# Attention weights summed over key tiles on GpSimd ahead of two matmuls with ones, in a one-core hybrid decoder layer

## What is computed

```
s = einsum('bhtd,bhsd->bhts', q, k) * w_ts
num = decay * einsum('bhtd,bhdv->bhtv', q, c_prev) + einsum('bhts,bhsv->bhtv', s, v)
den = decay * einsum('bhtd,bhd->bht', q, n_prev) + sum(s, axis=-1)
h = num / maximum(abs(den), exp(-m_t))
c_new = carry * c_prev + einsum('bhs,bhsd,bhsv->bhdv', g, k, v)
n_new = carry * n_prev + einsum('bhs,bhsd->bhd', g, k)
```

## Time and profile before

| | us |
|---|---|
| median of three runs | 1762.06 (1760.64 to 1764.90) |
| the profiled execution, its own time | 1765.68 |
| its span, first to last instruction | 1763.9 |
| TensorE busy | 1732.0 (98%) |
| VectorE busy | 1174.0 (67%) |
| ScalarE busy | 743.5 (42%) |
| GpSimd busy | 435.0 (25%) |
| mean granted clock of TensorE | 0.992 of full |

### The profile page before, as it was taken

How to read it: one execution, slowest core, us unless ns; L and a number is a source line. 1 busy time by engine, 2 the same in 40 slices (tenths; PEclk the granted TensorE clock), 3 DMA queues, 4 the chain that set the end, 5 groups by cost and what they waited for, 6 DMA issues and landing times.

```text
span 1763.9 us, 37199 instructions
## 1 busy us (share of the span) xinstructions
PE 1732.0 (98%) x13831; PEld 1717.0 (97%) x13831; DVE 1174.0 (67%) x1832; ACT 743.5 (42%) x867; POOL 435.0 (25%) x382
## 2 busy tenths in 40 slices
PE   8989999999999999999999999999999999999997
PEld 6889999999999999999999999999999999999997
DVE  3575765748576574857677887777545777777553
ACT  5533433443343344334344555544434333334443
POOL 3341421415142141514211222222000222222000
PEclk8999999999999999999999999999999999999998
DMA  7668678776857777686766566565666666666663
GB/s 185 161 158 205 161 210 195 192 199 177 208 153 212 188 201 193 184 202 161 201 176 180 161 188 179 173 181 170 181 185 182 179 178 178 179 176 178 178 173 107
DMA packets 591091, 318.79 MB, mean 181 GB/s; under 512 B 16771, under 2 KB 585603, under 8 KB 588907
## 3 DMA queue, kind: packets, MB, share of 16 engines
q1 hardware_dynamic: 576016, 292.66, 60.8%
q10 hardware_dynamic: 14555, 23.50, 5.2%
q0 software_dynamic: 432, 1.31, 0.3%
HBM read 305.07 MB, written 12.78 MB: 180 GB/s over the span
## 4 chain that ended last, share of the span: by engine, by line
PE 94%; DMA 2%; DVE 1%; ACT 1%; POOL 1%; issue 1%; SPq 0%; ACTq 0%; DVEq 0%; POOLq 0%
PE strip L1302 60%; PE strip L1307 30%; PE aux L1210 1%; PE aux L1395 1%; PE strip L1239 1%; PE aux L1399 1%; DMA x_tok<-in_x_prompt 1%; DMA scratch_q<-qkd 0%; PE aux L1256 0%; DVE w_lo L841 0%; PE aux L1371 0%; DMA rb<-scratch_rows 0%; PE strip L1249 0%; ACT w_hi L582 0%; PE aux L1408 0%
## 5 line engine op out<-in xcount | busy, mean ns | idle before, releaser
L841 DVE TENSOR_TENSOR w_lo<-w_raw,w_hi 128x1024 fp32r<-128x1024 f32 x556 | 715.4, 1289 | 382.5 <-ACT w_hi L582 379.9
L582 ACT ACTIVATE w_hi<-w_raw 128x1024 fp32r<-128x1024 f32 x560 | 592.7, 1060 | 883.6 <-PE strip L1307 846.6
L1302 PE MATMUL strip<-xh,w_hi 128*128 128x266 f32 (+2 forms) x3424 | 870.6, 288 | 1.5 <-ACT w_hi L582 1.5
L1302 PE MATMUL strip<-xl,w_hi 128*128 128x266 f32 (+2 forms) x3424 | 866.6, 287 | 0.0
L1302 PEld LDWEIGHTS strip<-xh,w_hi 128*128 128x128 f32 x3424 | 646.5, 189 | 2.3 <-ACT w_hi L582 1.6
L1302 PEld LDWEIGHTS strip<-xl,w_hi 128*128 128x128 f32 x3424 | 645.9, 189 | 0.3
L1307 PE MATMUL strip<-xh,w_lo 128*128 128x266 f32 (+2 forms) x3424 | 494.7, 287 | 3.5 <-DVE w_lo L841 3.5
L1307 PEld LDWEIGHTS strip<-xh,w_lo 128*128 128x128 f32 x3424 | 451.8, 189 | 3.9 <-DVE w_lo L841 3.9
L1302 PE MATMUL strip<-hh,w_hi 128*128 128x264 f32 x704 | 176.2, 286 | 0.0
L1302 PE MATMUL strip<-hl,w_hi 128*128 128x264 f32 x704 | 174.7, 283 | 0.0
L566 POOL TENSOR_TENSOR gg<-sg,cz 128x264 f32<-128x264 f32 x44 | 58.3, 1326 | 411.8 <-ACT sg L786 411.8
(11 more groups left out here) (284 smaller groups left out, 1247.3 us busy)
## 6 DMA issues: line engine op xcount, KB each, us to landing
w_raw<-in_w_in SPq DMA_DIRECT2D x256, 512.0 KB, 4.3
w_raw<-in_w_up SPq DMA_DIRECT2D x176, 512.0 KB, 4.0
w_raw<-in_w_down SPq DMA_DIRECT2D x64, 512.0 KB, 4.1
w_raw<-in_w_out SPq DMA_DIRECT2D x32, 512.0 KB, 4.1
w_raw<-in_w_down SPq DMA_DIRECT2D x32, 384.0 KB, 3.4
c_st<-in_state_mlstm_C ACTq DMA_DIRECT2D x8, 1024.0 KB, 11.1
out<-c_st ACTq DMA_DIRECT2D x8, 1024.0 KB, 6.9
rb<-scratch_rows ACTq DMA_DIRECT2D x8, 270.0 KB, 4.7
```

The source lines that it names most:

```text
L582: act.activation(w_hi[:, slot, :], w_raw[:, slot, :], ACT.Copy).then_inc(hi_done, 1)
L841: v.tensor_tensor(w_lo[:, slot, :], w_raw[:, slot, :], w_hi[:, slot, :].bitcast(f32), ALU.subtract).then_inc(lo_done, 1)
L1302: pe.matmul(bank[b][:, 0:c1 - c0], w_hi[:, slot, w], xt[:, k0 + k, c0:c1], start=(first and k == 0 and t == 0), stop=False)
```

## The change

On TensorE the three accumulating matmuls with ones over `pt`, and the one over `qp`, go. In their place GpSimd adds the key tiles of `pt` by query into `wx`, appends the product of sample queries and new `n` as 8 more columns, and splits the 266 columns into `p_hi` and `p_lo`, both fp32r. TensorE multiplies each with ones, after the matmuls for the new state, and waits for GpSimd before that. `p_hi` lies in the space of `arg`, `p_lo` in that of `wx`. The four small operations for the samples' `n` move from VectorE to GpSimd, three of them ahead of the wait for exp. The denominators of prompt and samples are taken in one pass of 266 columns, for which the rows in `rb` change order, and the three small operations at `i` = 22 go. `conv_state()` moves from behind the mask to the start of head 0's `back`, ahead of the wait for `rb`.

```diff
@@ gpsimd, back(n, first) @@
+                if first:
+                    conv_state()
                 g.wait_ge(rb_in, n * 16 + 16)
 ...
+                g.tensor_tensor(sn[:, :], scn[...], dec, ALU.mult).then_inc(sn_done, 1)
+                g.wait_ge(qkd_done, n * 3 + 3)
+                g.wait_ge(sn_done, n * 2 + 1)
+                g.tensor_tensor(sn[:, :], sn[:, :], qkd[:, :, 1], ALU.add).then_inc(sn_done, 1)
+                g.wait_ge(sn_done, n * 2 + 2)
+                g.tensor_tensor(n_new[...], sn[:, :], ones[:, 0:NS], ALU.mult).then_inc(n_kept, 1)
                 g.wait_ge(exp_done, n + 1)
                 g.tensor_tensor(g3[:, :], wx[:, WG:WN], scale_t[:, 0:3], ALU.mult).then_inc(g3_done, 1)
                 g.tensor_tensor(wx[:, 0:WG], wx[:, 0:WG], mask[:, 0:WG], ALU.mult).then_inc(masked, 1)
-                if first:
-                    conv_state()
 ...
                     g.tensor_tensor(cu[:, :], us[:, :], cgs[:, :], ALU.mult).then_inc(cu_done, 1)
                     if jj == 0:
+                        ps = n * PST
+                        g.wait_ge(p_done, n + 1)
+                        g.tensor_tensor(wx[:, Q1:PM], pt[:, Q1:PM], pt[:, W1:W2], ALU.add).then_inc(psum_step, 1)
+                        g.tensor_tensor(wx[:, 0:Q1], pt[:, 0:Q1], ones[:, 0:Q1], ALU.mult).then_inc(psum_step, 1)
+                        g.tensor_tensor(wx[:, PM:NM], q_t[:, PM:NM], sn[:, :], ALU.mult).then_inc(psum_step, 1)
+                        g.wait_ge(psum_step, ps + 1)
+                        g.tensor_tensor(wx[:, Q2:PM], wx[:, Q2:PM], pt[:, W2:WG], ALU.add).then_inc(psum_step, 1)
+                        g.wait_ge(psum_step, ps + 4)
+                        g.tensor_tensor(p_hi[:, :], wx[:, 0:NM], ones[:, 0:1].broadcast_to([P, NM]), ALU.mult).then_inc(psum_step, 1)
+                        g.wait_ge(psum_step, ps + 5)
+                        g.tensor_tensor(p_lo[:, :], wx[:, 0:NM], p_hi[:, :].bitcast(f32), ALU.subtract).then_inc(psum_step, 1)
@@ vector, back(n) @@
-                        v.tensor_tensor(den[:, 0:PM], aux[2][:, 0:PM], rb[:, R_EM:R_EM + PM], ALU.max)
+                        v.tensor_tensor(den[:, :], aux[2][:, 0:NM], rb[:, R_EM:R_EM + NM], ALU.max)
 ...
-                        v.reciprocal(rden[:, 0:PM], den[:, 0:PM])
+                        v.reciprocal(rden[:, :], den[:, :])
 ...
-                    if i == 13:
-                        (sn, sn, qp and n_new, four operations of 8 columns)
 ...
-                        (den, den and rden of the samples at i == 22, three operations of 8 columns)
@@ tensor, back(n) @@
-                        for a in range(3):
+                        for a in range(2):
                             for t, (c0, q0) in enumerate(((0, 0), (W1, Q1), (W2, Q2))):
-                                lhs = ones[:, :] if a == 2 else v_tok[:, t, a * P:(a + 1) * P]
-                                mm = pe.matmul(aux[a][:, q0:PM], lhs, pt[:, c0:c0 + PM - q0], start=(t == 0), stop=(t == 2))
-                        mm.then_inc(num_done, 1)
+                                pe.matmul(aux[a][:, q0:PM], v_tok[:, t, a * P:(a + 1) * P], pt[:, c0:c0 + PM - q0],
+                                          start=(t == 0), stop=(t == 2))
                         for t in range(3):
                             mm = pe.matmul(aux[3][:, 0:DV + 1], kg[:, t, :], v_tok[:, t, :], start=(t == 0), stop=(t == 2))
                         mm.then_inc(cn_done, 1)
+                        pe.wait_ge(psum_step, n * PST + PST)
+                        pe.matmul(aux[2][:, 0:NM], ones[:, :].bitcast(f32r), p_hi[:, :], start=True, stop=False)
+                        pe.matmul(aux[2][:, 0:NM], ones[:, :].bitcast(f32r), p_lo[:, :], start=False, stop=True)\
+                          .then_inc(num_done, 1)
                     if s == 10:
-                        pe.wait_ge(qn_done, n + 1)
-                        pe.matmul(aux[0][:, PM + 2 * NS:PM + 3 * NS], ones[:, :], qp[:, :], start=True, stop=True)
```

More of the change, by code:

```diff
@@ L67, in hybrid_decoder_step @@
     HST = 5
-    HSS = 4
+    PST = 6
     CH = 2
@@ L155, in hybrid_decoder_step @@
         kg = at("kg", [P, 3, DK])
+        arg_0 = cursor[0]
+        p_hi = at("p_hi", [P, NM], f32r)
+        cursor[0] = arg_0
         arg = at("arg", [P, WN])
+        wx_0 = cursor[0]
+        p_lo = at("p_lo", [P, NM], f32r)
+        cursor[0] = wx_0
         wx = at("wx", [P, WN])
@@ L286, in hybrid_decoder_step @@
             sem("scores_done"), sem("kv_turned"), sem("kv_done"), sem("vs_done"))
-        wsc_done, qkd_done, qkd_turned, qn_done, sn_done, sel_done = (
-            sem("wsc_done"), sem("qkd_done"), sem("qkd_turned"), sem("qn_done"), sem("sn_done"), sem("sel_done"))
+        wsc_done, qkd_done, qkd_turned, sn_done, sel_done = (
+            sem("wsc_done"), sem("qkd_done"), sem("qkd_turned"), sem("sn_done"), sem("sel_done"))
+        psum_step, n_kept = sem("psum_step"), sem("n_kept")
         sample_done, num_done, cn_done, pc_done = (
@@ L503, in back @@
                 g.tensor_tensor(qkd[:, :, 1], k_t[:, TP:NT], wsc[:, :], ALU.mult).then_inc(qkd_done, 1)
+                g.tensor_tensor(sn[:, :], scn[:, 2 * P:].rearrange("p (b h) -> p b h", b=NS)[:, :, bass.ds(n, 1)]
+                                .rearrange("p b a -> p (b a)"), dec, ALU.mult).then_inc(sn_done, 1)
+                g.wait_ge(qkd_done, n * 3 + 3)
+                g.wait_ge(sn_done, n * 2 + 1)
+                g.tensor_tensor(sn[:, :], sn[:, :], qkd[:, :, 1], ALU.add).then_inc(sn_done, 1)
+                g.wait_ge(sn_done, n * 2 + 2)
+                g.tensor_tensor(n_new[:, :, bass.ds(n, 1)].rearrange("p b a -> p (b a)"), sn[:, :], ones[:, 0:NS],
+                                ALU.mult).then_inc(n_kept, 1)
                 g.wait_ge(exp_done, n + 1)
@@ L542, in back @@
                     g.wait_ge(h_step, n * HST + HST)
[L543 removed]
+                    g.wait_ge(hs_step, n + 1)
                     g.tensor_tensor(so[:, :], so[:, :], h_t[:, jj, :], ALU.mult).then_inc(b_done, 1)
@@ L731, in back @@
                         act.wait_ge(h_step, n * HST + HST)
-                        act.wait_ge(hs_step, n * HSS + HSS)
-                        act.wait_ge(n_step, n * 2 + 2)
+                        act.wait_ge(hs_step, n + 1)
+                        act.wait_ge(n_kept, n + 1)
                         act.dma_start(rb[:, :], scratch_rows[bass.ds(n + 1, 1), :].broadcast_to([P, RW]))\
@@ L1003, in back @@
                         v.wait_ge(h_step, hs + 2)
-                        v.reciprocal(rden[:, 0:PM], den[:, 0:PM])\
+                        v.reciprocal(rden[:, :], den[:, :])\
                          .then_inc(h_step, 1)
@@ L1428, in _ @@
                     out_strip(i, q)
-            pe.wait_ge(n_step, 2 * H)
+            pe.wait_ge(n_step, H)
+            pe.wait_ge(n_kept, H)
             for t in range(NLAST):
```

25 lines of the change are left out of this document (7 added, 18 removed).

## The result

The changed kernel takes 1759.56 us (median of 20 runs, 1754.99 to 1762.44); the kernel before takes 1762.53 beside it (20 runs, 1760.64 to 1764.90). The ratio is 0.9979, with a 95% interval of 0.9972 to 0.9985: 3.0 us less in the medians. 12 us were forecast, and the time lies outside the range of 1743 to 1756.5. One execution of a later kernel (2624 us) and one of the kernel before (4341 us) ran in a far slower state and are left out, which moves a median by under 0.2 us.

A forecast was written before the change was run, and what follows sets the result against it. TensorE, busy 98% of the span, was taken as the bound. 5.2 us in heads 1 to 7 plus 6.6 in head 0 took 1765.68 to 1753.9; less 3.6 to a median gave 1750 us, range 1743 to 1756.5.

The forecast's parts named there:

- The steps: Savings summed over the whole kernel: 5.2 us in heads 1 to 7 plus 6.6 in head 0, 11.8 us.
- the 1753.9 worked out for it: Forecast time of the profiled execution: 1765.68 us before the change, less 11.8 us.
- the step from that execution to a median: Whole kernel: the median was 3.6 us below the profiled execution; the same difference was assumed after the change, giving 1750.
- In heads 1 to 7, where nothing else bounds, 7 x 0.74 = 5.2 us: TensorE, heads 1 to 7: matmuls with ones removed, two fp32r ones added, net 0.74 us a head, 5.2 us.
- up to 3.4: VectorE, heads 1 to 7: comes up to 3.4 us earlier, its w_lo no longer behind the removed block.
- 4.2 + 2.4 = 6.6: Head 0: 4.2 us from the earlier c_st load and qkd store, 2.4 from VectorE's removed block, 6.6 us.
- rival B: Head 0: weight loads crowd the c_st load, qkd's store lands as before; 1754.5, or 1756.9 with nothing gained there; chance 0.14.
- near 5: Head 0, TensorE's wait at L1408 for the samples' sum: stays near 5 us, and the clock falls as before.
- the late end of 198.9: GpSimd, head 1: six key-tile operations end at 198.9 if w_lo holds them up, before TensorE comes at 201.8.
- rival C: Each head: TensorE waits for GpSimd before the two matmuls with ones; 1767 us or more at 10 us; chance 0.06.
- rival D: Head 0: conv-state sums don't come early, the chain to rb slips; about 1757 to 1760 us; chance 0.08.

The follow-up runs named there:

- experiment above: Kernel before plus conv-state sums first, head 0's c_st load at i = 9, samples' matmuls behind strip 11; matmuls with ones kept: 1751.48 us.
- both edits: Changed kernel with the samples' matmuls behind strip 11 and head 0's c_st load at i = 9 instead of 11: 1744.82 us, ratio 0.9899.

## Why the prediction was wrong

The forecast of 1750 misses 1759.56 by 9.6 us. Three parts make that up. The steps gave 6.7 us instead of 11.8 (5.1 missing). The execution came 1.6 us sooner to head 0's scores (69.81 to 68.21), which second profiles of the two kernels don't repeat (68.77 and 69.07), so its own time came out 3.5 above the 1753.9 worked out for it (5.1 - 1.6). And the step from that execution to a median, 3.6 us downwards, went 2.2 upwards: 5.8 (another 0.3 was rounding).

**Failed: "In heads 1 to 7, where nothing else bounds, 7 x 0.74 = 5.2 us".** The price was sound: L1398 now takes 1.72 us for 12 instructions and the two new matmuls 0.12 and 0.13, in the chain that ended last in head 3:

```profile
396.35 1.72 PE aux L1398 x12
...
399.47 0.12 PE aux L1406
399.59 0.13 PE aux L1407
```

That is 2.62 + 0.12 - 1.72 - 0.25 = 0.77 us, and heads free of waits are 0.83 shorter (experiment above). The error is in "nothing else bounds". TensorE came to the samples' matmul 0.8 us earlier (41.74 to 40.95 behind the scores), and the sum that it waits for hardly did.

The slack had been read from one row, of one head, and too large. The forecast took 0.7 us, from the sum's end at 225.8 to the end of L1404 at 226.52. But L1408 is the one that needs the sum, it starts at 226.38 in head 1, and the starts behind a late sum show that it can begin 0.15 us after the sum at the earliest. That leaves 0.4 us in head 1. In head 2 of the kernel before there was none: the sum ends at 328.66 and L1408 starts 0.14 behind it, already bound. The rows of the kernel before are L1408 of head 1, then the sum and L1408 of head 2; behind them L1414 of the changed kernel's head 1, whose sum ends at 219.81:

```profile
226.38 0.59 PE L1408 MATMUL aux<-sel,sacc 128*128 128x8 f32 x4
...
328.23 0.43 DVE L1039 TENSOR_TENSOR sacc<-sacc 128x256 f32<-128x256 f32 x1
...
328.80 0.58 PE L1408 MATMUL aux<-sel,sacc 128*128 128x8 f32 x4
```

```profile
219.96 0.58 PE L1414 MATMUL aux<-sel,sacc 128*128 128x8 f32 x4
```

Over heads 1 to 6 the slack of the kernel before is 0.42, 0, 0.21, 0.38, 0.03 and 0.21 us, 1.25 in all. Their sums end 0.65 us earlier in the changed kernel, again in all. That makes 1.9 us, and 1.91 is what the six heads gave. I let the thin slack pass because VectorE would be "up to 3.4" earlier, once its block was gone. In head 1 it is 0.2: the sum ends 41.0 us behind the scores (41.2 before). The time of the block went into operations held up by GpSimd's `kv` and `c_st` steps and its decay product: two `w_lo` take 4.10 us above, where 2.4 is their price alone, and `cv` 3.90. Putting the block back moved the sum by only 0.4 us. That GpSimd's steps pace the stretch fits both; no run made them shorter. With no slack, each delay of `vg` is passed on too. In head 3 it lands after 4.2 us instead of 2.8, and the decay product starts 17.7 behind the scores instead of 15.2:

```profile
194.03 3.60 POOL L546 TENSOR_TENSOR c_st<-c_st,qkd_g 128x2048 f32<-128x2048 f32 x1 [1.11 <-DMA vg<-scratch_v]
...
399.96 3.60 POOL L546 TENSOR_TENSOR c_st<-c_st,qkd_g 128x2048 f32<-128x2048 f32 x1 [3.60 <-DMA vg<-scratch_v]
```

That head is 102.89 long. Of the 5.4 us that the six heads could give with the samples' matmuls later (614.12 - 608.76), the wait took back 3.5.

**Mis-sized: head 0's "4.2 + 2.4 = 6.6".** The sum ended 4.6 us earlier relative to the scores (52.5 to 47.9). The pieces, each relative to the scores:

- The load of `c_st` was issued at 8.2 instead of 14.8, 6.6 earlier and not 5.2. Of the start I took 1 us off for a busier landing; the store landed at 21.1 instead of 24.4, so 3.3 was left, not 4.2, and the landing cost 3.1 us. Half of rival B was true in this execution; with a load as fast as in two of the later profiles less of it would have been.
- From the landing to the decay product it was 2.9 us and is now 4.2: `vg`, 3.72 us, was not in the sum. It cost 1.3.
- From the decay product to the sum's end it is 2.7 us less (25.3 to 22.6): near the 2.4 taken for the block, but not for the reason given. The forecast had the next `w_lo` meet the decay product instead. In fact VectorE had done its two `w_lo` by then, and the denominators ran beside the decay product, not held up. With the block put back the same stretch takes 22.6 us as well, since the block ran ahead of the decay product there. So the size is luck in part: what counts is which operation meets the decay product, and that depends on when `vg` lands.
- Behind the wait, TensorE works 4.4 us at the lower clock instead of 3.4: 0.4 us more. The wait itself is 6.8, not "near 5".

So 4.6 - 0.4 = 4.2 for head 0. That its wait stays, and that the chain counts, was right.

**Right.** GpSimd's six operations end 14.1 us behind the scores; the late end of 198.9 is 14.3. In head 1 they and the wait of the decay product are:

```profile
187.39 0.77 POOL L528 TENSOR_TENSOR cu<-us,cgs 128x268 f32<-128x268 f32 x1 [4.11 <-DVE cgs L876]
188.12 1.48 POOL L533 TENSOR_TENSOR wx<-pt 128x144 f32<-128x144 f32 x1
...
190.41 0.63 POOL L539 TENSOR_TENSOR p_hi<-wx,ones 128x266 fp32r<-128x266 f32 x1
191.12 1.79 POOL L541 TENSOR_TENSOR p_lo<-wx,p_hi 128x266 fp32r<-128x266 f32 x1
```

TensorE doesn't wait for them (rival C falls: they end at 14.1, it comes at 16.8), and 1.1 us later GpSimd takes up the decay product without delay. The conv-state sums run from 61.36 to 69.07, before `rb` is there at 69.9, so rival D falls as well.

**Open.** From head 0's scores on, the pairs of profiles differ by 6.7 and 5.8 us, the medians by 3.0 and 4.8. The runs of the changed kernel spread over 7.5 us and those with the early `c_st` alone over 6.8 (five runs); with both edits it is 2.7 (four runs), and 1.3 in the last version with the matmuls with ones (five runs). A head bound by the chain behind the load of `c_st` passes on how long that takes, and the profiles show it at 8.5 to 13.8 us with the same queue ahead of it. In the changed kernel's two profiles the clock was also below full for 4.4 and about 6.4 us of work after the wait of head 0. Both fit the spread, but the profiles are one execution each, and no run separates them. The scores of head 0 started at 67.5 to 69.8 us between profiles, whatever the kernel. That an execution lies 3.6 us above the median in one kernel and 2.2 below it in the other is a spread that the forecast carried over as a fixed difference.

## What to carry to other kernels

Before counting a saving on the busiest engine, list for each of its later waits, in every repetition, how long before the wait's end the producer had been done, and compare that slack with the saving. Here it was 0 to 0.4 us against a saving of 0.8, so most of the saving went into the wait. Read it from starts, since a short wait is in no list. An engine relieved of work may give nothing earlier if it then stands in the way of another. And a stall can be cheapest to cure at its consumer: moving the samples' matmul by one strip gave 5 us in the kernel before and 12.5 in the changed one, where the whole rework alone gave 3 to 5.

## What the runs showed of the hardware

- VectorE and GpSimd held each other up by whole operations where both read large tiles. A step of `cv` over 258 columns took 3.90 us beside a GpSimd operation over 2048 columns, 0.49 without; GpSimd's subtraction of 266 columns (`p_lo`) took 1.79 us beside a `w_lo` in head 1 of the changed kernel, and 0.81 in head 0 of the kernel with VectorE's block. The Trainium skill ("GPSIMD Engine Reference", section Specifications) names the shared SBUF interfaces and the VectorE instructions with two SBUF inputs that contend for them; the trace agrees, and shows that the one held up can wait for the other's whole length.
- A store of 12 KB behind a 1 MB load in ScalarE's queue landed within 1 us of the load in all eleven profiles in which the load was still under way. It took 6.9 to 8.5 us where both were issued late in head 0 (four profiles), 10.7 to 11.7 or, in two profiles, 7.0 and 7.1 where both were issued earlier, as in the changed kernel (seven), and 5.1 to 6.3 where the load had landed before the store went out (three).
- After the waits for `sacc` of head 0, 4.6 and 6.8 us, TensorE's clock was at the lower level (1.2 GHz) for 3.4 and 4.4 us of the work that followed. The length of a wait alone didn't decide. The clock stayed at its full level behind 2.6 us ahead of `w_lo` in the kernel before, and behind 2.0 us at L1414 with the early `c_st`. The lower level followed 2.5 us ahead of `w_lo` in the second profile of the kernel before, 1.9 us in the kernel before with the samples later (0.66 in the mean of 105 to 110 us), and 1.6 us in head 3 of the kernel with more work on GpSimd.
